# A two-block transformer layer on one core: modulation sums between output tiles, the last square summed by TensorE, the last tiles added from PSUM, and two narrow projections in one unit

## What is computed

```python
h = h + rmsnorm(mix, norm_mix_post)                 # "mix_post" and then "ffn_pre"
y = (gelu(gate) * val) @ w_ffn_out                  # ffn_out of the first block
x = h + rmsnorm(y, norm_ffn_post)                   # "ffn_post"
mod = silu(c) @ w_ada + b_ada                       # 6 parts of 1024
sh_m, sc_m, g_m, sh_f, sc_f, g_f = split(mod, 6)
h = rmsnorm(x, norm_mix_g) * (1 + sc_m) + sh_m      # "mix2"
proj = h @ w_in                                     # u, qi, ki (64), wi (8), q, k, v, ga, gb
...                                                 # indexer: relu(qi . ki) weighted by wi
x = x + g_m * (merged @ w_out)                      # out2
h = rmsnorm(x, norm_ffn_g) * (1 + sc_f) + sh_f      # "ffn2"
x = x + g_f * ((silu(a) * b) @ w_ffn_out)           # ffn_out2
return rmsnorm(x, norm_final_g)                     # "final"
```

## Time and profile before

| what | value |
|---|---|
| median of three runs | 1575.24 us (1573.3 to 1578.36) |
| the profiled execution's own time | 1569.78 us |
| its span in the trace | 1567.9 us |
| TensorE (PE) busy | 1496.6 us, 95% |
| VectorE (DVE) busy | 814.4 us, 52% |
| ScalarE (ACT) busy | 593.8 us, 38% |
| GpSimd (POOL) busy | 552.8 us, 35% |
| HBM read | 151.89 MB, 98 GB/s over the span |

### The profile page before, as it was taken

One profiled execution on the slowest core, in us unless ns is written; L12 is line 12 of the kernel. 1 busy time (PEld: TensorE's weight loads), 2 busy tenths in 40 slices (PEclk: granted clock), 3 DMA queues, 4 the chain that ended last, 5 costly groups with the idle time before them and its releaser, 6 DMA issues.

```text
span 1567.9 us, 20753 instructions
## 1 busy us (share of the span) xinstructions
PE 1496.6 (95%) x8722; PEld 1268.1 (81%) x8722; DVE 814.4 (52%) x1083; ACT 593.8 (38%) x945; POOL 552.8 (35%) x229
## 2 busy tenths in 40 slices
PE   7999899989999999999899989999888999999996
PEld 7988788878999999887688757777776888888885
DVE  4732444436455555876599479962634334332122
ACT  5432333544333333222422364455444323333231
POOL 3321111132344434555044322323442445444441
PEclk9999999989999999999799999999998999999998
DMA  6210111111222224875122211112132323322222
GB/s 228 82 62 34 67 66 41 42 68 68 85 92 95 95 86 169 291 258 216 37 98 94 81 54 68 65 43 81 67 108 89 114 104 111 134 94 94 100 102 81
DMA packets 43772, 155.32 MB, mean 99 GB/s; under 512 B 4992, under 2 KB 5632, under 8 KB 43680
## 3 DMA queue, kind: packets, MB, share of 16 engines
q1 hardware_dynamic: 43104, 151.51, 27.3%
q10 hardware_dynamic: 576, 2.49, 0.5%
HBM read 151.89 MB, written 2.10 MB: 98 GB/s over the span
## 4 chain that ended last, share of the span: by engine, by line
PE 75%; DVE 6%; ACT 2%; issue 1%; POOL 0%; DVEq 0%; ACTq 0%
PE G L430 68%; DVE scb L1926 1%; DVE small L1925 1%; PE B L811 1%; PE B L407 1%; PE B L899 1%; PE B L923 1%; PE B L868 1%; PE B L400 0%; PE G L685 0%; DVE yab L2001 0%; PE G L910 0%; DVE ub L1520 0%; DVE rstd L1507 0%; DVE yab L2000 0%
## 5 line engine op out<-in xcount | busy, mean ns | idle before, releaser
L387 POOL TENSOR_TENSOR wlo<-raw,whi 128x1024 fp32r<-128x1024 f32 x225 | 552.6, 2458 | 987.4 <-ACT whi L1007 987.2
L430 PE MATMUL G<-uhi,whi 128*128 128x258 f32 (+3 forms) x1904 | 532.7, 332 | 29.1 <-DVE wlo L1531 9.3
L430 PE MATMUL G<-ulo,whi 128*128 128x258 f32 (+3 forms) x1904 | 521.9, 326 | 0.0
L430 PE MATMUL G<-uhi,wlo 128*128 128x258 f32 (+3 forms) x1904 | 521.3, 326 | 0.0
L430 PEld LDWEIGHTS G<-uhi,whi 128*128 128x128 f32 x1904 | 321.0, 191 | 89.3 <-issue 41.7
L430 PEld LDWEIGHTS G<-uhi,wlo 128*128 128x128 f32 x1904 | 322.0, 191 | 30.0
L430 PEld LDWEIGHTS G<-ulo,whi 128*128 128x128 f32 x1904 | 321.3, 191 | 28.2
L1007 ACT ACTIVATE whi<-raw 128x1024 fp32r<-128x1024 f32 x227 | 239.1, 1054 | 179.6 <-DMA raw<-wstream 179.5
L430 PE MATMUL G<-yhi,whi 128*128 128x512 f32 x352 | 139.0, 395 | 0.0
L430 PE MATMUL G<-yhi,wlo 128*128 128x512 f32 x352 | 138.9, 395 | 0.0
L430 PE MATMUL G<-ylo,whi 128*128 128x512 f32 x352 | 138.9, 395 | 0.0
(11 more groups left out here) (280 smaller groups left out, 1555.1 us busy)
## 6 DMA issues: line engine op xcount, KB each, us to landing
raw<-wstream SPq DMA_DIRECT2D x227, 512.0 KB, 3.2
ada_in<-ada SPq DMA_DIRECT2D x40, 512.0 KB, 5.8
ada_late<-ada SPq DMA_DIRECT2D x8, 512.0 KB, 3.4
h<-hT SPq DMA_DIRECT2D x8, 264.0 KB, 3.3
out<-res SPq DMA_DIRECT2D x8, 256.0 KB, 2.1
biasn<-bias SPq DMA_DIRECT2D x2, 960.0 KB, 8.2
biasn<-bias ACTq DMA_DIRECT2D x2, 960.0 KB, 4.7
scan_keep<-scanm SPq DMA_DIRECT2D x1, 528.0 KB, 6.4
```

The lines of the kernel that those rows point to most:

```text
L387: pool.tensor_tensor(wlo[:, i, :], raw[:, i, :], whi[:, i, :].bitcast(F32), ALU.subtract)\
L430: ins = pe.matmul(dst[:, x, 0:xw], w[:, slot, b * P:(b + 1) * P], u[:, k, off + x0:off + x0 + xw], start=(first and i == 0 and j == 0), st ...
```

## The change

It has five parts.

1. The one-column sums of the modulation (`mod_part`): before, parts 0 and 1 stand behind the last tile of `ffn_out`, and parts 2 to 4 behind the sum of `ffn_post`. Now parts 0 and 1 stand behind tiles 3 and 5 of `ffn_out` (and write another PSUM bank), part 2 behind the sum of `ffn_post`, part 3 behind the sums of `mix2`, part 4 behind tile 3 of `u2`. VectorE adds the bias in two steps.
2. For the norms in `ADDED`, VectorE adds only the first seven squares. TensorE sums that tile (`sum_added`) and the eighth square (`sum_last`) into the same place.
3. In `out2` and `ffn_out2` VectorE reads the finished tile from PSUM, scales it and adds it to `h` in one instruction; ScalarE's copy is gone.
4. The indexer's key (64 columns, which stood twice in its unit) and head weights (8 columns, a unit of their own) share one unit. The second copy of the key is made by a DMA in SBUF, issued by ScalarE.
5. ScalarE: in `ffn_out` the rounding of unit 3c + 5 now stands behind the square of tile c, not ahead of it. Two loads of the function table (in `squares`) are gone.

The diff, cut to its core:

```diff
-         "u2", 8), ("qi2", 4), ("ki2", 1), ("wi2", 1), ("q2", 4), ...
+         "u2", 8), ("qi2", 4), ("ki2", 1), ("q2", 4), ...
...
+            def sum_added(norm):
+                nh, hw = norm_halves(NORMS[norm][1])
+                pe.wait_ge(s["sq_added"], (KD - 2) * (ADDED.index(norm) + 1))
+                for x in range(nh):
+                    pe.matmul(B4[:, x, 0:hw], ones[:, :], scratch(norm)[2][:, x * hw:(x + 1) * hw],
+                              start=True, stop=False)
+            def sum_last(norm):
+                r, W = NORMS[norm]
+                nh, hw = norm_halves(W)
+                pe.wait_ge(s["sq_done"], KD * (r + 1))
+                for x in range(nh):
+                    last = pe.matmul(B4[:, x, 0:hw], ones[:, :],
+                                     scratch(norm)[0][:, (KD - 1) % square_depth(norm), x * hw:(x + 1) * hw],
+                                     start=False, stop=True)
+                last.then_inc(s["ss_ps"], 1)
...
+            def residual_free(name, c):
+                if c >= 2:
+                    pe.wait_ge(s["h_done"], KD * (2 if name == "out2" else 3) + c - 1)
+                else:
+                    tile_free(T0[name] + c)
...
-                    if after:
-                        after(c)
+                    if name == "ffn_out" and c in (3, 5):
+                        mod_part((c - 3) // 2, ada_acc[(c - 3) // 2])
...
-            sums("ffn_post")
-            for part in range(2, 5):
-                mod_part(part, ada_acc[part])
+            sum_added("ffn_post")
+            sum_last("ffn_post")
+            mod_part(2, ada_acc[2])
             sums("mix2")
+            mod_part(3, ada_acc[3])
             two_tiles(U0["u2"], T0["u2"], lambda k: split_ready("mix2", k), W=SEQ)
             for i in range(2, 8):
                 fm_tile(U0["u2"] + i, T0["u2"] + i, 0, SEQ)
+                if i == 3:
+                    mod_part(4, ada_acc[4])
...
                 act.activation(m2[:, c, :], G[:, t % 2, 0, :], ACT.Copy).then_inc(s["evac_done"], 1)
-                hi_through(U0["ffn_out"] + 3 * c + RING + 1)
                 act.wait_ge(s["evac_done"], t + 1)
                 square("ffn_post", c, m2[:, c, :])
+                hi_through(U0["ffn_out"] + 3 * c + RING + 1)
...
+            act.activation(ki2[0:64, :], G[0:64, t % 2, 0, :], ACT.Copy)
+            act.activation(wi2T[64:72, :], G[64:72, t % 2, 0, :], ACT.Copy).then_inc(s["evac_done"], 1)
+            hi_through(n + RING - 1)
+            act.wait_ge(s["evac_done"], t + 1)
+            act.dma_start(ki2[64:128, :], ki2[0:64, :]).then_inc(s["ki_copied"], 16)
...
+            def add_residual(name, per, scale, norm):
+                before = KD * (2 if name == "out2" else 3)
+                for c in range(KD):
+                    dve.wait_ge(s["unit_used"], U0[name] + per * (c + 1))
+                    dve.scalar_tensor_tensor(h[:, c, META:T], G[:, (T0[name] + c) % 2, 0, :], scale(c), h[:, c, META:T],
+                                             ALU.mult, ALU.add).then_inc(s["h_done"], 1)
+                    if c >= 2:
+                        add_square(norm, c - 1)
+                dve.wait_ge(s["h_done"], before + KD)
```

More of the change, by code:

```diff
@@ L68 @@
     T0[_n] = _at
-    _at += {"ffn_out": 8, "ffn_out2": 8, "proj2": 16}.get(_n, _w)
+    _at += {"ffn_out": 8, "ffn_out2": 0, "proj2": 16, "out2": 0}.get(_n, _w)
 MIXED = [("g", 0), ("g", 1), ("g", 2), ("g", 3), ("q", 0), ("k", 0), ("v", 0),
@@ L396, in sums @@
                 nh, hw = norm_halves(W)
-                if norm in ADDED:
-                    pe.wait_ge(s["sq_added"], (KD - 1) * (ADDED.index(norm) + 1))
-                    for x in range(nh):
-                        last = pe.matmul(B4[:, x, 0:hw], ones[:, :], scratch(norm)[2][:, x * hw:(x + 1) * hw],
-                                         start=True, stop=True)
-                    last.then_inc(s["ss_ps"], 1)
-                    return
                 for k in range(KD):
@@ L471, in _ @@
             pe.wait_ge(s["ones_in"], 16)
-            sums("mix_pre")
+            sum_added("mix_pre")
+            sum_last("mix_pre")
             half_tile(B4[:, 2:4], q_last, 1)
@@ L778, in _ @@
                 fm_tile(U0["w_o"] + i, T0["w_o"] + i, FT0, FT, order=GLA_FIRST)
-            sums("mix_post")
+            sum_added("mix_post")
+            sum_last("mix_post")
             sums("ffn_pre")
@@ L1025, in square @@
                     if norm in ADDED:
[L1026 removed]
+                        act.wait_ge(s["sq_added"], (KD - 2) * ADDED.index(norm) + k + 1 - depth)
                     else:
@@ L1501, in add_square @@
                 depth = square_depth(norm)
-                before = (KD - 1) * ADDED.index(norm)
+                before = (KD - 2) * ADDED.index(norm)
                 dve.wait_ge(s["sq_done"], KD * r + k + 1)
@@ L1804, in _ @@
             na_low(4)
-            for k in range(1, KD):
+            for k in range(1, KD - 1):
                 add_square("mix_post", k)
```

89 lines of the change are left out of this document (40 added, 49 removed).

## The result

The changed kernel takes 1559.49 us (median of six runs, 1557.38 to 1565.92) against 1574.27 for the kernel before in the same session (six runs, 1570.9 to 1578.36). The ratio is 0.9907, 95% interval 0.9882 to 0.9932, so 14.8 us by the medians. A later session with six more runs gave 1558.65 and 0.9916 (0.99 to 0.9931). The profiled execution took 1558.69, its span is 1556.9: 11.1 and 11.0 less than before.

The account below looks back on a forecast made before the run. PE's list bounds the kernel from end to end (busy 95%). The terms 1.0 - 1.2 - 3.7 - 5.6 - 2.1 - 1.9 + 0.3 = -13.2 us take 1575.24 to 1562.0; range 1556.5 to 1568.

Parts of the forecast that it names:

- B: mix_post, end of w_o: the last square summed by PE without VectorE's last add brings Ln earlier, -1.2 us.
- C: ffn_post, mix2 and the modulation: moved one-column sums and the shorter square relay, together -3.7 us.
- A: mix_pre: a second group of sums between products of a busy PE, hidden by nothing, +1.0 us.
- T': End of ffn_out's last product with parts 0 and 1 in PE's dense stream, 3.6 us later than before.
- R1: Rival: PE's lower clock takes part back in the last sums and u2's cold start; -8.2 us, 1567.0; 14%.
- D: Key and head weights: one unit less saves one tile's time on PE ahead of the first score, -5.6 us.
- R2: Rival: VectorE's convolution holds the index stage's first score, limiting the unit's gain; -9 us, 1566; 5%.
- E: End of out2: VectorE's residual straight from PSUM and PE's sum of the last square bring Ln earlier, -2.1 us.
- F: End of ffn_out2: the same residual from PSUM and last-square sum with GpSimd quiet, -1.9 us.
- G: ScalarE's order in ffn_out: the rounding behind the square leaves no room at tile 2, +0.3 us over all tiles.
- R4: Rival: ScalarE's new order in ffn_out starves PE, units 3 us late at six tiles; +18 us, 1580; 3%.
- R3: Rival: the moved one-column sums lower PE's clock amid products, 2 us for each of three groups; 1568.0; 4%.

Follow-up runs that it names:

- order_back: The changed kernel with ScalarE's rounding of unit 3c + 5 of ffn_out ahead of the square of tile c again; 1561.46 us, ratio 0.9934.
- split_later: The changed kernel with GpSimd's split of the third unit of ffn_in and u2 delayed until VectorE has added the last normed tile; 1556.42 us, ratio 0.9891.
- adds_back: The changed kernel with all eight squares added by VectorE and one group of sums in all five norms; 1563.05 us, ratio 0.9945.
- mod_back: The changed kernel with all one-column sums where they stood before the change; 1564.6 us, ratio 0.9941.
- the second trace: Profile of the changed kernel run again without any edit, in a later session; 1558.65 us, ratio 0.9916.
- mod_gaps: The changed kernel with one-column part 1 moved ahead of part 2 and part 4 behind part 3, both in TensorE's waits; 1559.58 us, ratio 0.9904.
- unit_only: The kernel before with only the key and the head weights put in one unit; 1567.8 us, ratio 0.9969.
- unit_back: The changed kernel with the key and the head weights in two units again; 1568.21 us, ratio 0.9972.
- all_four: The changed kernel with no one-column sums among tiles, later third-unit split, squares added right behind residuals, mix_pre as before; 1553.9 us, ratio 0.9883.

## Why the prediction was right

The predicted 1562.0 lies 2.5 us above the measured median, and -13.2 between what the medians (-14.8) and the profiled executions (-11.1) give. The direction and the largest term were reasoned and came true. That the number is so close is in part luck: by the traces the terms come to 0.9 - 0.6 - 2.2 - 5.6 - 2.3 - 1.8 + 0 = -11.6, since B and C gave 2.1 us less than forecast. The medians differ by 3.2 us more than these terms, and nothing in the runs says from where. Point by point, by the traces:

- **A**: +1.0, and 0.9 measured, from the start of the first group to Ln (2.04 us, with one group 1.15). The +1.0 of the whole stretch is no better proof, since it is 18.0 to 19.4 us in the ten traces with two groups and 17.3 to 18.5 in the four with one.
- **B**: -1.2, and -1.15 to Ln, of which 0.4 was the clock in the trace of before. Half of the 1.15 went at once: the step that failed is that the term ends at Ln and puts nothing on the way behind it. With Ln earlier by one add, VectorE's first scaled tiles meet GpSimd's split, and Ln to Ln grew by 0.55. order_back and split_later show it. From tile to ffn_pre's Ln the part is worth 0.6 us against the trace of before, and 0.2 against adds_back.
- **C**: -3.7, and 3.5 - 8.35 + 1.8 + 0.8 = -2.2 measured. The square's relay (Ln at T' + 2.45) was 2.49. "From Ln to Ln 14.56" was 15.25: the same split. The cold start of u2, which stood in R1 alone, took 0.8: of the 2.9 us ahead at mix2's Ln, 2.1 were left at u2's first tile. The reason given for C was right in its places and wrong in its worth: mod_back shows that the move itself wins nothing (0.8 us lost, 2.1 against the second trace), since what stands among tiles costs its full length (parts 0 and 1 3.5, part 4 1.8). What was left of C came with the clock. mod_gaps shows where parts 1 and 4 cost nothing, 3.9 us.
- **D**: -5.6. Measured 5.6 locally from both sides. R2 falls, but one reading was wrong: 3.8 of the 8.88 us of idle time were to be used and 4 to 6 to be left, and 3.32 were left. VectorE's taps follow the tiles of u2, which part 4 delays as it delays PE (the last tile is copied at 814.39, before at 814.68; the last tap is 0.3 earlier too). So the whole 5.56 us of D come out of the idle time, and unit_only, without part 4, has the same 3.32.
- **E**: -2.1, and -2.3; 3.74 and not 3.9 us from tile to Ln. The way there was partly another: PE's two groups stand one behind the other once VectorE's add 6 is late, and the square of tile 7 (1166.82) no longer decides. The rule of the Trainium skill, "SBUF — State Buffer", section "Who interferes with whom" (two SBUF inputs contend with GpSimd's reads, one does not), fits in direction: the residual with one PSUM input took 0.75 beside GpSimd, the add with two SBUF inputs 1.00, where it takes 0.68 with GpSimd quiet. A full block until the split's end at 1166.18 would have made it 1.14; ends on GpSimd are rough, so the trace can't say whether the block was full.
- **F**: -1.9, and -1.8 (5.25 to 3.42 us).
- **G**: +0.3, and 0: no wait for `wlo` in ffn_out, and the tiles 0 to 3 kept their distance of 15.3 us. R4 falls, R3 too: the tile behind a moved part came 1.8 us later and no more (17.12 us instead of 15.33), and the windows behind it (680 to 696 and 712 to 728) have a clock of 1.00.
- **R1** (the lower clock takes part back) happened in C and not in B, E and F of the changed kernel. The lower clock also goes with what unit_back lost beyond its edit, and with what all_four lost behind q2. Waits are not all that stands ahead of it: PE was busy throughout when the clock fell again in mod_back.

Not foreseen were the later first product (+1.4), within the 9.3 to 11.3 us of all traces, and the -1.2 behind q2, which goes with the clock and which no edit explains.

## What to carry to other kernels

When a relay between two engines gets shorter by a step, look at what a third engine does in the microseconds that the relay moves into: the 0.5 to 0.8 us lost here twice were won back by delaying one GpSimd instruction into a wait of VectorE. Work that TensorE does for a later need costs its whole length among products, and nothing in a wait that is long enough. And where whole runs of one program differ by 8.5 us, judge an edit by its own stretch, measured between the same instructions, and the whole by many runs.
